# Two transformer blocks in split float32: low halves of the weight tiles written over the raw tiles, eight slots instead of four

## The chip, the cores and the metric

The kernel runs on one core of one Trainium2 chip. The metric is the device time of one execution in microseconds. Engines are named as in the profile: PE (TensorE; PEld is its weight load), DVE (VectorE), ACT (ScalarE), POOL (GpSimd), SP (SyncE, which here only issues DMAs).

## What is computed

The input x has 256 tokens of width 1024. A first block adds three attentions (differential, latent with top-k, block) and a squared-ReLU feed-forward; two further layers add a gated convolution and a retention each. Cut to what matters:

```
u = rmsnorm(x) * (1 + scale1) + shift1           # 1024 wide
p = u @ w_in                                     # 6312 columns: q, k, v, gates ...
merged = g0 * (diff_attn @ w_a) + g1 * (dsa @ w_b) + g2 * (moba @ w_c)
x = x + gate1 * (merged @ w_o)
h = square(relu(u2 @ w_ff1));  x = x + gate2 * (h @ w_ff2)      # 1024 -> 4096 -> 1024
for l in range(2):                               # two mixing layers
    p = rms_norm(x) @ w_in_2[l]                  # 1024 -> 8192: conv b, c, x, z; retention q, k, v, z
    x = x + rms_norm(concat(conv, retention) @ w_out_2[l])
```

All weights and inputs are float32.

## The kernel before

**Units.** Every weight matrix is cut into 291 units of 128 x 1024 (eight blocks of 128 x 128), in one stream in the order of use: 0 to 26 projections, 27 to 50 gates, 51 to 58 the three branch outputs, 59 to 66 w_o, 67 to 98 w_ff1, 99 to 130 w_ff2, then 80 units for each mixing layer (from 131 and from 211): 32 for the retention, 32 for the convolution (163 to 194, 243 to 274), 16 for the output. Activations lie transposed, 128 rows of 256 tokens.

**Split.** A weight tile `raw` is split into `w_hi` (ACT copies it to the matmul's rounded float32) and `w_lo = raw - w_hi`. Activations are split the same way. A unit is then eight times three matmuls, hi by hi, hi by lo, lo by hi (lines 544 to 546, and 562 to 564 in `first_units`, which runs two or three units side by side behind a norm).

**Rings.** `raw` has four slots of two tiles each (`RAW_PAIRS`), `w_hi` and `w_lo` four slots of one tile each (`SLOTS`). For unit c:

- SP loads the pair p = c // 2 (`load`, line 393). From p = 4 on it waits until the low halves of the pair four back are made.
- ACT makes the high half (`high`, line 996) when the tile has landed and unit c-4 is done. It is called at the end of ACT's work on unit c-4: `high(None, c + SLOTS)`.
- The low half (`low`) is made by POOL (line 455, four quarters of 128 x 256) and, where c % 4 == 3 and for unit 4, by DVE (line 1397, one instruction). It waits for the high half and for unit c-4.
- PE waits for both halves, and for the PSUM bank (`taken`).

```
            act.wait_ge(raw_in[(c // 2) % RAW_PAIRS], lin(g, 16, 16 * (c // 2 // RAW_PAIRS + 1)))
            if c >= SLOTS:
                act.wait_ge(S["unit_done"], lin(g, 8, c - SLOTS + 1))
```

**Order around it.** Each engine runs one program written out in order, with semaphores between them. ACT and DVE step from unit to unit: wait for `unit_done`, take the result out of PSUM, do the step's share of attention, norms, gates or activation, then `high` or `low` for a unit ahead. In the convolution stage ACT's fourth step of a group of four first waits for DVE's `zr` to take a tanh (line 1355) and then calls `high`. POOL does almost nothing but low quarters. SP does the loads in order; ten of the loads of `ada` (modulation weights) at the start and the bias table go through it as well, 14 more `ada` loads through ACT's queue.

Of the kernel before, what the change touches and what calls it, by code (L numbers as in the profile page):

```python
# [32 lines left out]
P = 128  # L33
# [33 lines left out]
SLOTS = 4  # L67
# [7 lines left out]
RAW_PAIRS = 4  # L75
# [50 lines left out]
def _build(nc, ctx, xT, weights, ada, c_row, cols, dl, relb, onehot, ident_d, flip_d, cmask_d, decay, positions, w_uv, out):  # L126
# [173 lines left out]
    names = """ident_in tab_in dl_in pos_in start_pool pool_own raw_in0 raw_in1 raw_in2 raw_in3 small_in x_in tab_out bias_in decay_in stored  # L300
# [15 lines left out]
    raw_in = [S[f"raw_in{i}"] for i in range(RAW_PAIRS)]  # L316
# [72 lines left out]
    def _(sp):  # L389
# [3 lines left out]
        def load(g, p):  # L393

            src = weights[p] if g is None else weights[bass.ds(g * 4 + p, 1)].rearrange("o p n -> p (o n)")
            if p >= RAW_PAIRS:
                n = 2 * p - 2 * RAW_PAIRS + 2
                sp.wait_ge(S["lo_pool"], lin(g, 8, n))
                if n % 4 == 0 and p > 5:
                    sp.wait_ge(S["lo_dve"], lin(g, 8, n))  # L400
                if p == 6:
                    sp.wait_ge(S["lo_first"], 1)
            both = 2 * p + 1 < UNITS
            width = (2 if both else 1) * KC * P
            sp.dma_start(raw[:, p % RAW_PAIRS, 0:width], src[:, 0:width]).then_inc(raw_in[p % RAW_PAIRS], 16)

# [5 lines left out]
        load(None, 0)  # L412
        ada_load(sp, 3)
        load(None, 1)
# [5 lines left out]
        load(None, 2)  # L420
        load(None, 3)
# [5 lines left out]
        load(None, 4)  # L427
        ada_load(sp, 8)
        ada_load(sp, 9)
        load(None, 5)  # L430
# [6 lines left out]
        for p in range(6, 8):  # L437
            load(None, p)
        n_loops = (UNITS // 2 - 8) // 4
        with sp.Fori(0, n_loops) as g:  # L440
            for i in range(4):
                load(g, 8 + i)
        for p in range(8 + 4 * n_loops, (UNITS + 1) // 2):
            load(None, p)
# [9 lines left out]
    def _(pool):  # L454
        def low(g, c):
            if g is None and c <= 4:
                if c == 4:
                    return
            elif c % 4 == 3:
                return  # L460
            pool.wait_ge(S["hi_ready"], lin(g, 8, c + 1))
            if c >= SLOTS:
                pool.wait_ge(S["unit_done"], lin(g, 8, c - SLOTS + 1))
            r = raw[:, (c // 2) % RAW_PAIRS, (c % 2) * KC * P:(c % 2 + 1) * KC * P]
            s = c % SLOTS
# [39 lines left out]
        lows(12, U_LAYER + LAYER_UNITS + SLOTS)  # L505
        x_adds(0)
        lows(U_LAYER + LAYER_UNITS + SLOTS, UNITS)
# [484 lines left out]
    def _(act):  # L992
# [206 lines left out]
        for n, (kind, q) in enumerate(BR_UNITS):  # L1199
            act.wait_ge(S["unit_done"], U_BR + n + 1)  # L1200
            high(None, U_BR + n + SLOTS)
# [27 lines left out]
        for j in range(KC):  # L1229
            o = O_WO + j  # L1230
            act.wait_ge(S["unit_done"], U_WO + j + 1)
            high(None, U_WO + j + SLOTS)
# [9 lines left out]
        def up_turn(g, base):  # L1242
            for i in range(8):
# [5 lines left out]
                high(g, c + SLOTS)  # L1249
# [14 lines left out]
        for j in range(KC):  # L1264
            for q in range(4):
                c = U_F2 + 4 * j + q
                act.wait_ge(S["unit_done"], c + 1)
                if c + 1 < U_LAYER:
                    high(None, c + SLOTS)
# [8 lines left out]
        high(None, U_LAYER + SLOTS - 1)  # L1278

        for l in range(LAYERS):  # L1280
# [4 lines left out]
            def a_turn(g, n0):  # L1285
# [34 lines left out]
                for i in range(8):  # L1320
# [10 lines left out]
                    high(g, c0 + i + SLOTS)  # L1331
# [13 lines left out]
            def b_turn(g, n0):  # L1345
                c0, o0 = uA + 32 + 8 * n0, oA + 32 + 8 * n0
                for e in range(2):
                    n = 2 * n0 + e
                    for i in range(4):
# [6 lines left out]
                        high(g, c0 + ii + SLOTS)  # L1356
# [15 lines left out]
            for j in range(KC):  # L1372
                for q in range(2):
# [8 lines left out]
                    high(None, c + SLOTS)  # L1382
# [10 lines left out]
    def _(dve):  # L1393
# [3 lines left out]
        def low(g, c):  # L1397
# [281 lines left out]
        for c in range(N_QKV + N_GATE):  # L1679
# [18 lines left out]
            if c:  # L1698
                low(None, c + SLOTS)
# [23 lines left out]
        for n, (kind, q) in enumerate(BR_UNITS):  # L1723
# [22 lines left out]
            low(None, U_BR + n + SLOTS)  # L1746
# [17 lines left out]
        for j in range(KC):  # L1764
# [4 lines left out]
            low(None, U_WO + j + SLOTS)  # L1769
# [10 lines left out]
        def up_turn(g, base):  # L1780
            for i in range(8):
# [7 lines left out]
                low(g, c + SLOTS)  # L1789
# [37 lines left out]
        for j in range(KC):  # L1827
            for q in range(4):
# [9 lines left out]
                low(None, c + SLOTS)  # L1838
# [8 lines left out]
        for l in range(LAYERS):  # L1847
# [4 lines left out]
            def a_turn(g, n0):  # L1852
# [35 lines left out]
                for i in range(8):  # L1888
# [5 lines left out]
                    if i == 3:  # L1894
                        if n0 == 0:
                            low(g, c0 + i + SLOTS)
# [3 lines left out]
                    if i != 3 or n0:  # L1900
                        low(g, c0 + i + SLOTS)
# [41 lines left out]
            def b_turn(g, n0):  # L1943
# [5 lines left out]
                for e in range(2):  # L1949
# [6 lines left out]
                    for i in range(4):  # L1956
# [29 lines left out]
                        low(g, c0 + ii + SLOTS)  # L1986
# [19 lines left out]
            for j in range(KC):  # L2006
                for q in range(2):
# [4 lines left out]
                    if j < KC - 1 or q == 0:  # L2012
                        low(None, c + SLOTS)
# [4 lines left out]
            low(None, uA + 79 + SLOTS)  # L2018
# [164 lines left out]
```

## Time and profile before

| | |
|---|---|
| time, median of 3 runs | 992.1 us (991.79, 992.1, 993.59) |
| profiled execution, its own time | 999.17 us |
| profiled execution, span | 997.3 us |
| mean granted TensorE clock | 0.987 |
| PE busy | 945.3 us (95%), 7758 matmuls |
| DVE / ACT / POOL busy | 656.8 / 493.3 / 727.8 us |
| DMA | 185.2 MB, 186 GB/s on the mean |

All times are microseconds from the start of the span. "Idle before" is the time in which an engine waited, with the line that released it; "issue" is waiting for nothing that the profile shows. Matmuls overlap, so the time from one's start to the next one's is what a matmul costs, not its own 0.28 us.

### The profile page before, as it was taken

How to read it: one execution, taken by the hardware profiler on the slowest of the kernel's cores; microseconds unless marked ns; L12 is line 12 of the kernel's file. 1: busy time of each engine (PE TensorE's matmuls, PEld its weight loads, DVE VectorE, ACT ScalarE, POOL GpSimd, SP SyncE). 2: the span in 40 equal slices, each digit the busy share in tenths (PEclk: the TensorE clock that was granted, in tenths of full speed). 3: DMA queues.
4: the chain of work that ended last, by engine and by line, in shares of the span. 5: the costliest groups of instructions: out<-in, count | busy, mean ns of one | idle time of the engine just before them, and what ended most of it. 6: DMA issues, size and time to landing. Idle time of an engine off the chain costs nothing. (4 is left out here: it accounts for less than half of the span.)

```text
span 997.3 us, 21947 instructions
## 1 busy us (share of the span) xinstructions
PE 945.3 (95%) x7758; PEld 920.4 (92%) x7758; DVE 656.8 (66%) x1097; ACT 493.3 (49%) x811; POOL 727.8 (73%) x894
## 2 busy tenths in 40 slices
PE   6999899999889999999999999999978999999996
PEld 6898789998888999999899999999978999999996
DVE  4979996756887654432566668885455666788823
ACT  3445567654446555454444454444543444644451
POOL 1585666668668888787676659999935666799993
PEclk9999999999999999999999999999988999999998
DMA  9985554646444546555344435555404444445531
GB/s 367 398 318 186 196 204 181 249 141 265 150 164 170 203 176 253 196 195 185 127 170 169 164 131 176 204 178 202 175 37 150 151 164 168 169 170 176 201 108 43
DMA packets 28222, 185.20 MB, mean 186 GB/s; under 512 B 3027, under 2 KB 5504, under 8 KB 6272
## 3 DMA queue, kind: packets, MB, share of 16 engines
q1 hardware_dynamic: 25832, 167.93, 46.4%
q10 hardware_dynamic: 2328, 16.40, 4.5%
q8 instruction: 43, 0.70, 0.3%
q14 instruction: 19, 0.16, 0.0%
HBM read 183.26 MB, written 1.07 MB: 185 GB/s over the span
## 5 line engine op out<-in xcount | busy, mean ns | idle before, releaser
L470 POOL TENSOR_TENSOR w_lo<-raw,w_hi 128x256 fp32r<-128x256 f32 x876 | 718.3, 856 | 244.0 <-ACT w_hi L1004 241.4
L544 PE MATMUL mm<-u_hi,w_hi 128*128 128x256 f32 x1600 | 460.4, 288 | 8.3 <-issue 8.1
L545 PE MATMUL mm<-u_lo,w_hi 128*128 128x256 f32 x1600 | 447.4, 280 | 0.0
L546 PE MATMUL mm<-u_hi,w_lo 128*128 128x256 f32 x1600 | 447.2, 279 | 0.0
L1004 ACT ACTIVATE w_hi<-raw 128x1024 fp32r<-128x1024 f32 x291 | 306.2, 1058 | 145.1 <-PE mm L546 140.3
L544 PEld LDWEIGHTS mm<-u_hi,w_hi 128*128 128x128 f32 x1600 | 304.3, 190 | 16.5 <-issue 15.8
L545 PEld LDWEIGHTS mm<-u_lo,w_hi 128*128 128x128 f32 x1600 | 302.4, 189 | 2.0 <-issue 1.9
L546 PEld LDWEIGHTS mm<-u_hi,w_lo 128*128 128x128 f32 x1600 | 302.8, 189 | 0.0
L1409 DVE TENSOR_TENSOR w_lo<-raw,w_hi 128x1024 fp32r<-128x1024 f32 x72 | 99.9, 1387 | 61.8 <-ACT w_hi L1004 59.2
L544 PE MATMUL mm<-mix_hi,w_hi 128*128 128x256 f32 x256 | 71.0, 277 | 1.7 <-DVE mix_lo L1979 1.7
L544 PE MATMUL mm<-h_hi,w_hi 128*128 128x256 f32 x256 | 71.9, 281 | 0.0
L545 PE MATMUL mm<-h_lo,w_hi 128*128 128x256 f32 x256 | 71.9, 281 | 0.0
L546 PE MATMUL mm<-h_hi,w_lo 128*128 128x256 f32 x256 | 71.9, 281 | 0.0
L546 PE MATMUL mm<-mix_hi,w_lo 128*128 128x256 f32 x256 | 70.7, 276 | 0.0
L545 PE MATMUL mm<-mix_lo,w_hi 128*128 128x256 f32 x256 | 70.7, 276 | 0.0
L544 PEld LDWEIGHTS mm<-mix_hi,w_hi 128*128 128x128 f32 x256 | 48.1, 188 | 2.2 <-DVE mix_lo L1979 2.1
L544 PEld LDWEIGHTS mm<-h_hi,w_hi 128*128 128x128 f32 x256 | 49.2, 192 | 0.0
L545 PEld LDWEIGHTS mm<-mix_lo,w_hi 128*128 128x128 f32 x256 | 48.1, 188 | 0.0
L546 PEld LDWEIGHTS mm<-mix_hi,w_lo 128*128 128x128 f32 x256 | 48.1, 188 | 0.0
L545 PEld LDWEIGHTS mm<-h_lo,w_hi 128*128 128x128 f32 x256 | 48.0, 188 | 0.0
L546 PEld LDWEIGHTS mm<-h_hi,w_lo 128*128 128x128 f32 x256 | 48.0, 188 | 0.0
L578 PE MATMUL mm<-ident,ones 128*128 128x128 f32 x264 | 35.1, 291 | 9.1 <-DMA ident<-ident_d 9.1
(292 smaller groups left out, 1354.0 us busy)
## 6 DMA issues: line engine op xcount, KB each, us to landing
raw<-weights SPq DMA_DIRECT2D x145, 1024.0 KB, 4.8
ada_raw<-ada ACTq DMA_DIRECT2D x14, 1024.0 KB, 5.2
ada_raw<-ada SPq DMA_DIRECT2D x6, 1024.0 KB, 12.3
ada_more<-ada SPq DMA_DIRECT2D x4, 1024.0 KB, 12.8
bias<-tab_scratch SPq DMA_DIRECT2D x1, 1536.0 KB, 9.2
dec<-decay ACTq DMA_DIRECT2D x1, 1536.0 KB, 6.9
x<-xT SPq DMA_DIRECT2D x1, 1024.0 KB, 10.8
out<-x SPq DMA_DIRECT2D x4, 256.0 KB, 2.2
```

Source lines behind the costliest of these rows:

```text
L470: ins = nc.gpsimd.tensor_tensor(w_lo[:, s, at], r[:, at], hi[:, at], ALU.subtract)
L544: nc.tensor.matmul(dst, wh, rhs_hi(k), start=a, stop=False)
L545: nc.tensor.matmul(dst, wh, rhs_lo(k), start=False, stop=False)
L546: i = nc.tensor.matmul(dst, wl, rhs_hi(k), start=False, stop=b)
L578: nc.tensor.matmul(mm[o % 4][:, 0:P], ones[:, :], ident[:, :], start=True, stop=True)
L1004: A(w_hi[:, c % SLOTS, :], r, ACT.Copy).then_inc(S["hi_ready"], 1)
L1409: ins = V.tensor_tensor(w_lo[:, s, :], r, w_hi[:, s, :].bitcast(F32), ALU.subtract)
```

## The change

`raw` and `w_lo` become one piece of memory of eight tiles: the low half is subtracted in place. `w_hi` gets eight slots too. Of a partition, the three tensors took 8 + 4 + 4 tiles of 4 KB before, and take 8 + 8 tiles now, 64 KB both times; the small fillers of 32 bytes between them move behind them. ACT makes the high half five units ahead (`HI_AHEAD`), the low halves are still called four units ahead (`LO_AHEAD`) but wait for the high half alone. Each unit's tile is loaded by a DMA of its own, 512 KB, with one semaphore per slot, as soon as the unit eight back is done. At the start, ACT makes high half 4 before the first unit is done, and the loads of units 8 and 9 stand behind two `ada` loads instead of ahead of them.

```diff
-SLOTS = 4
+SLOTS = 8
+HI_AHEAD = 5
+LO_AHEAD = 4
...
-RAW_PAIRS = 4
...
-    keep("step_raw", [P, 8])
-    raw = keep("raw", [P, RAW_PAIRS, 2 * KC * P])
-    keep("step_w", [P, 8])
+    with ExitStack() as early:
+        raw = tile_in(early, "raw", [P, SLOTS, KC * P])
+    w_lo = keep("w_lo", [P, SLOTS, KC * P], F32R)
     w_hi = keep("w_hi", [P, SLOTS, KC * P], F32R)
-    w_lo = keep("w_lo", [P, SLOTS, KC * P], F32R)
-    keep("step_vec", [P, 8])
+    keep("step_vec", [P, 24])
...
-        def load(g, p):
-
-            src = weights[p] if g is None else weights[bass.ds(g * 4 + p, 1)].rearrange("o p n -> p (o n)")
-            if p >= RAW_PAIRS:
-                n = 2 * p - 2 * RAW_PAIRS + 2
-                sp.wait_ge(S["lo_pool"], lin(g, 8, n))
-                if n % 4 == 0 and p > 5:
-                    sp.wait_ge(S["lo_dve"], lin(g, 8, n))
-                if p == 6:
-                    sp.wait_ge(S["lo_first"], 1)
-            both = 2 * p + 1 < UNITS
-            width = (2 if both else 1) * KC * P
-            sp.dma_start(raw[:, p % RAW_PAIRS, 0:width], src[:, 0:width]).then_inc(raw_in[p % RAW_PAIRS], 16)
+        def load(g, c):
+
+            if g is None:
+                src = weights[c // 2][:, c % 2 * KC * P:(c % 2 + 1) * KC * P]
+            else:
+                src = weights[bass.ds(g * 4 + c // 2, 1)].rearrange("o p n -> p (o n)")\
+                    [:, c % 2 * KC * P:(c % 2 + 1) * KC * P]
+            if c >= SLOTS:
+                sp.wait_ge(S["unit_done"], lin(g, 8, c - SLOTS + 1))
+            sp.dma_start(raw[:, c % SLOTS, :], src).then_inc(raw_in[c % SLOTS], 16)
...
-        load(None, 2)
-        load(None, 3)
+        for c in range(4, 8):
+            load(None, c)
...
-        load(None, 4)
         ada_load(sp, 8)
         ada_load(sp, 9)
-        load(None, 5)
+        for c in range(8, 11):
+            load(None, c)
         sp.wait_ge(S["tab_out"], 16)
...
             pool.wait_ge(S["hi_ready"], lin(g, 8, c + 1))
-            if c >= SLOTS:
-                pool.wait_ge(S["unit_done"], lin(g, 8, c - SLOTS + 1))
-            r = raw[:, (c // 2) % RAW_PAIRS, (c % 2) * KC * P:(c % 2 + 1) * KC * P]
-            s = c % SLOTS
-            hi = w_hi[:, s, :].bitcast(F32)
+            r = raw[:, c % SLOTS, :]
+            lo = w_lo[:, c % SLOTS, :]
+            hi = w_hi[:, c % SLOTS, :].bitcast(F32)
...
-                ins = nc.gpsimd.tensor_tensor(w_lo[:, s, at], r[:, at], hi[:, at], ALU.subtract)
+                ins = nc.gpsimd.tensor_tensor(lo[:, at], r[:, at], hi[:, at], ALU.subtract)
...
-            act.wait_ge(raw_in[(c // 2) % RAW_PAIRS], lin(g, 16, 16 * (c // 2 // RAW_PAIRS + 1)))
-            if c >= SLOTS:
-                act.wait_ge(S["unit_done"], lin(g, 8, c - SLOTS + 1))
-            r = raw[:, (c // 2) % RAW_PAIRS, (c % 2) * KC * P:(c % 2 + 1) * KC * P]
-            A(w_hi[:, c % SLOTS, :], r, ACT.Copy).then_inc(S["hi_ready"], 1)
+            act.wait_ge(raw_in[c % SLOTS], lin(g, 16, 16 * (c // SLOTS + 1)))
+            A(w_hi[:, c % SLOTS, :], raw[:, c % SLOTS, :], ACT.Copy).then_inc(S["hi_ready"], 1)
...
+        high(None, 4)
         for c in range(N_QKV + N_GATE):
             act.wait_ge(S["unit_done"], c + 1)
             (qkv_evac if c < N_QKV else act_gate)(c)
-            high(None, c + SLOTS)
+            high(None, c + HI_AHEAD)
...
             dve.wait_ge(S["hi_ready"], lin(g, 8, c + 1))
-            if c >= SLOTS:
-                dve.wait_ge(S["unit_done"], lin(g, 8, c - SLOTS + 1))
-            r = raw[:, (c // 2) % RAW_PAIRS, (c % 2) * KC * P:(c % 2 + 1) * KC * P]
             s = c % SLOTS
-            ins = V.tensor_tensor(w_lo[:, s, :], r, w_hi[:, s, :].bitcast(F32), ALU.subtract)
+            ins = V.tensor_tensor(w_lo[:, s, :], raw[:, s, :], w_hi[:, s, :].bitcast(F32), ALU.subtract)
```

Every other call of `high` with `+ SLOTS` becomes `+ HI_AHEAD` and every call of `low` becomes `+ LO_AHEAD`, at the same place of its program.

## Rows read from the trace of the kernel before

**Rows 1.** The page's costliest groups: busy us, mean ns of one, idle us before them

```profile
L470 POOL TENSOR_TENSOR w_lo<-raw,w_hi 128x256 fp32r<-128x256 f32 x876 | 718.3, 856 | 244.0 <-ACT w_hi L1004 241.4
```

**Rows 2.** Waits of the whole span, by who waited: us in total, times, longest

```profile
POOL w_lo L470 <- ACT w_hi L1004: 241.4, 105, 19.1
...
DVE w_lo L1409 <- ACT w_hi L1004: 59.2, 33, 5.3
...
PE mm L544 <- issue: 9.4, 12, 3.5
...
SPq L405 <- POOL w_lo L470: 492.6, 96, 10.1
```

**Rows 3.** Timeline of PE: start, duration, in brackets idle before

```profile
53.09 0.36 PE L544 MATMUL mm<-u_hi,w_hi 128*128 128x256 f32 x1 [0.19 <-issue]
...
277.91 0.28 PE L546 MATMUL mm<-m_hi,w_lo 128*128 128x256 f32 x1
...
279.47 0.36 PE L544 MATMUL mm<-m_hi,w_hi 128*128 128x256 f32 x1 [1.28 <-issue]
...
304.35 0.28 PE L546 MATMUL mm<-u_hi,w_lo 128*128 128x256 f32 x1
...
304.81 0.36 PE L544 MATMUL mm<-u_hi,w_hi 128*128 128x256 f32 x1 [0.18 <-issue]
...
307.50 0.28 PE L546 MATMUL mm<-u_hi,w_lo 128*128 128x256 f32 x1
...
308.32 0.36 PE L544 MATMUL mm<-u_hi,w_hi 128*128 128x256 f32 x1 [0.54 <-issue]
...
311.02 0.28 PE L546 MATMUL mm<-u_hi,w_lo 128*128 128x256 f32 x1
...
312.63 0.35 PE L544 MATMUL mm<-u_hi,w_hi 128*128 128x256 f32 x1 [1.33 <-issue]
...
936.45 0.36 PE L544 MATMUL mm<-u_hi,w_hi 128*128 128x256 f32 x1
```

**Rows 4.** Timeline of POOL up to the starts of units 66 and 74

```profile
265.32 14.05 POOL L470 TENSOR_TENSOR w_lo<-raw,w_hi 128x256 fp32r<-128x256 f32 x12 [6.51 <-ACT w_hi L1004]
301.11 11.42 POOL L470 TENSOR_TENSOR w_lo<-raw,w_hi 128x256 fp32r<-128x256 f32 x12 [11.15 <-ACT w_hi L1004]
```

**Rows 5.** Timeline of ACT, high halves of units 63, 64, 71 and 72

```profile
260.91 1.06 ACT L1004 ACTIVATE w_hi<-raw 128x1024 fp32r<-128x1024 f32 x1 [3.98 <-PE mm L546]
...
264.18 1.06 ACT L1004 ACTIVATE w_hi<-raw 128x1024 fp32r<-128x1024 f32 x1 [1.90 <-PE mm L546]
...
298.44 1.06 ACT L1004 ACTIVATE w_hi<-raw 128x1024 fp32r<-128x1024 f32 x1
...
299.96 1.06 ACT L1004 ACTIVATE w_hi<-raw 128x1024 fp32r<-128x1024 f32 x1
```

**Rows 6.** Stretches: us; busy (count) of PE, PEld, DVE, ACT, POOL; PEclk, DMA share, GB/s

```profile
250.00:262.00 12.00, 9.36 (x62) 8.62 (x61) 9.53 (x20) 4.67 (x8) 6.89 (x8) 0.86 0.28 102
312.63:473.82 161.19, 161.19 (x1368) 161.19 (x1369) 75.11 (x102) 84.90 (x132) 133.68 (x174) 1.00 0.56 200
602.66:673.82 71.16, 69.98 (x603) 69.06 (x601) 61.26 (x94) 32.18 (x43) 69.44 (x77) 1.00 0.52 185
683.34:715.98 32.64, 32.64 (x290) 32.64 (x289) 14.30 (x15) 16.63 (x24) 29.72 (x38) 1.00 0.56 198
868.03:939.27 71.24, 70.80 (x602) 70.41 (x601) 60.79 (x94) 32.16 (x43) 68.89 (x77) 1.00 0.52 185
```

**Rows 7.** Timelines of POOL and PE in the convolution stage

```profile
643.99 10.90 POOL L470 TENSOR_TENSOR w_lo<-raw,w_hi 128x256 fp32r<-128x256 f32 x12 [0.54 <-ACT w_hi L1004]
...
648.11 0.36 PE L544 MATMUL mm<-u_hi,w_hi 128*128 128x256 f32 x1 [0.28 <-issue]
```

**Rows 8.** The instructions that write x on POOL: ns min/median/max

```profile
L492 POOL TENSOR_TENSOR x<-x,o_out x8: 722/725/922, 725.5 to 993.9; 128x256 f32<-128x256 f32 x8
```

**Rows 9.** Loads of raw between 300 and 700 us, from issue to landing

```profile
DMA to landing us min/median/max: 4.6/4.8/8.9
```

More of the change, by code:

```diff
@@ L315, in _build @@
     S = {n: sem(n) for n in names}
-    raw_in = [S[f"raw_in{i}"] for i in range(RAW_PAIRS)]
+    raw_in = [S[f"raw_in{i}"] for i in range(SLOTS)]
     taken = [S[f"taken{i}"] for i in range(4)]
@@ L412, in _ @@
         load(None, 0)
+        load(None, 1)
         ada_load(sp, 3)
-        load(None, 1)
+        load(None, 2)
+        load(None, 3)
         ada_load(sp, 4)
@@ L435, in _ @@
             .then_inc(S["bias_in"], 16)
-        for p in range(6, 8):
-            load(None, p)
-        n_loops = (UNITS // 2 - 8) // 4
+        for c in range(11, 16):
+            load(None, c)
+        n_loops = (UNITS - 16) // 8
         with sp.Fori(0, n_loops) as g:
[L441 to L444, printed above, removed]
+            for i in range(8):
+                load(g, 16 + i)
+        for c in range(16 + 8 * n_loops, UNITS):
+            load(None, c)
         for q in range(4):
@@ L1200, in _ @@
             act.wait_ge(S["unit_done"], U_BR + n + 1)
-            high(None, U_BR + n + SLOTS)
+            high(None, U_BR + n + HI_AHEAD)
             if n < 2:
@@ L1231, in _ @@
             act.wait_ge(S["unit_done"], U_WO + j + 1)
-            high(None, U_WO + j + SLOTS)
+            high(None, U_WO + j + HI_AHEAD)
             if j in (2, 4):
@@ L1268, in _ @@
                 if c + 1 < U_LAYER:
-                    high(None, c + SLOTS)
+                    high(None, c + HI_AHEAD)
                 if c == U_F2 + SIN_AT:
@@ L1277, in _ @@
             square_x(2, j, x[:, j, :], scale=col("norm_final", j))
-        high(None, U_LAYER + SLOTS - 1)
+        high(None, U_LAYER + HI_AHEAD - 1)
         for l in range(LAYERS):
@@ L1330, in a_turn @@
                         vt_copy(vt_at.index(i))
-                    high(g, c0 + i + SLOTS)
+                    high(g, c0 + i + HI_AHEAD)
                     if i in (5, 7):
@@ L1381, in _ @@
                             .then_inc(taken[o % 4], 1)
-                    high(None, c + SLOTS)
+                    high(None, c + HI_AHEAD)
             root(3 + 2 * l)
@@ L1698, in _ @@
             if c:
-                low(None, c + SLOTS)
+                low(None, c + LO_AHEAD)
             lam_steps(c)
@@ L1745, in _ @@
                 o += 1
-            low(None, U_BR + n + SLOTS)
+            low(None, U_BR + n + LO_AHEAD)
             if kind == "c":
@@ L1768, in _ @@
                 .then_inc(taken[o % 4], 1)
-            low(None, U_WO + j + SLOTS)
+            low(None, U_WO + j + LO_AHEAD)
             if j:
@@ L1788, in up_turn @@
                     .then_inc(S["hl_ready"], 1)
-                low(g, c + SLOTS)
+                low(g, c + LO_AHEAD)
         up_turn(None, 0)
@@ L1837, in _ @@
                         row_lo(2, j, nf_pre[:, j:j + 1])
-                low(None, c + SLOTS)
+                low(None, c + LO_AHEAD)
                 if q == 0 and j:
@@ L1895, in a_turn @@
                         if n0 == 0:
-                            low(g, c0 + i + SLOTS)
+                            low(g, c0 + i + LO_AHEAD)
                         decayed(0)
@@ L1900, in a_turn @@
                     if i != 3 or n0:
-                        low(g, c0 + i + SLOTS)
+                        low(g, c0 + i + LO_AHEAD)
                     if i >= 6:
@@ L1985, in b_turn @@
                             dve.wait_ge(S["yc_ready"], lin(g, 2, 8 * l + n + 1))
-                        low(g, c0 + ii + SLOTS)
+                        low(g, c0 + ii + LO_AHEAD)
                         if ii == 0 and n0 == 0:
@@ L2012, in _ @@
                     if j < KC - 1 or q == 0:
-                        low(None, c + SLOTS)
+                        low(None, c + LO_AHEAD)
                 if l == 0:
@@ L2017, in _ @@
             variance(n_out)
-            low(None, uA + 79 + SLOTS)
+            low(None, uA + 79 + LO_AHEAD)
             dve.wait_ge(S["rstd_ready"], n_out + 1)
```

10 lines of the change are left out of this document (5 added, 5 removed).

## The prediction

> **What bounds the kernel now.** I read the engine table first: TensorE is busy 945.3 of 997.3 us, so only what lets PE start a unit earlier, or makes its matmuls follow each other faster, can move the time by much. A unit is one 128x1024 weight tile: 24 matmuls, preceded by one ScalarE instruction that makes its high half and by its low half, four GpSimd instructions of 856 ns mean in three units of four, one VectorE instruction in the fourth [rows 1]. Three low tiles take GpSimd 12 x 0.856 = 10.3 us of the 11 us or so that four units take PE. The reader should see there that GpSimd is the next engine behind PE, with under 10% to spare.
>
> Next the waits. PE is hardly ever held in a way that the list can name: 9.4 us in 12 waits stand as "issue", that is, nothing that the profile shows [rows 2]. GpSimd meanwhile waits 241.4 us for high halves, VectorE 59.2 us, and SyncE waits 492.6 us for low halves before it may load [rows 2]. The loads run far ahead, so their waiting costs nothing.
>
> The "issue" waits can be named by laying the PE and GpSimd timelines on each other. GpSimd's run of 12 instructions (units 64, 65, 66) ends at 265.32 + 14.05 = 279.37, and PE, which had started its last matmul of unit 65 at 277.91, starts unit 66 at 279.47 [rows 3, 4]. The run for units 72, 73, 74 ends at 301.11 + 11.42 = 312.53 and PE starts unit 74 at 312.63; the starts at 304.81 and 308.32 are of units 72 and 73 [rows 3, 4]. So each of these is a wait for the low half, and what made it late is the high half before it: GpSimd had stood idle 6.51 and 11.15 us for it, because with four slots ScalarE may not write it before the unit four back is done.
>
> Last the pace. Matmuls of a unit follow each other at one of two steps, and stay with it until something disturbs them. From 312.63 to 473.82 are 57 units, 1368 matmuls, with no stop: 161.19 / 1368 = 0.1178 us. From 683.34 to 715.98 are 12 units, 288 matmuls (the view counts two that reach over the edge): 32.64 / 288 = 0.1133 us. Both at granted clock 1.00 [rows 6]. A unit is 2.83 us at the slow step and 2.72 at the fast one.
>
> **The change part by part.**
>
> *Work.* The count of every compute instruction stays. One 1024 KB load for two units becomes two of 512 KB: 146 issues become 291, on SyncE, which mostly waits. TensorE's instructions don't change.
>
> *High halves five units ahead instead of four.* The last unit done that ScalarE waits for before it makes tile c is c-5 instead of c-4. Where PE is fed with slack this costs and brings nothing. It counts in these places:
>
> (a) Unit 66. High half 64 starts at 264.18, behind unit 60. It moves into the slot of 63, at 260.91, 3.27 us earlier [rows 5]. GpSimd's run then starts about 262.05 instead of 265.32 and ends at 276.1, before PE needs it. The wait is 279.47 - 277.91 less one step of 0.12: **1.4 us** gained.
>
> (b) Units 72 to 74. High half 72 moves from 299.96 to the slot of 71, at 298.44: 1.52 us [rows 5]. GpSimd runs without a gap behind it, so low half 74 is ready 1.52 us sooner, and unit 74 starts at 311.1 instead of 312.63. The waits are 0.34 + 0.71 + 1.49 = 2.5 us (304.81 - 304.35, 308.32 - 307.50, 312.63 - 311.02, less a step each). **1.5 us** gained; about 1.0 us of waiting at unit 74 is left.
>
> (c) The convolution stage of both layers. There ScalarE makes the high half of every fourth unit (170, 174, ...) behind a tanh that waits for VectorE, GpSimd waits 0.54 us for it, and runs 10.90 us of the next 11.45 [rows 7]; PE waits in turn (648.11) [rows 7]. The change makes that high half one unit sooner, ahead of the tanh, and puts the one behind the tanh on VectorE's tile. GpSimd then needs 10.90 us in four units of 11.31 (slow step) or 10.87 (fast step). From 602.66 to 673.82 are 25 units in 71.16 us, in the other layer 71.24 [rows 6]. At the slow step and with no wait they take 25 x 24 x 0.1178 = 70.70: 0.46 + 0.54 = **1.0 us**. It isn't the 3 us or so of waits, since a wait here often put PE on the fast step, and PE enters this stage on the slow one. At best PE takes the fast step and GpSimd bounds it: 25/4 x 10.95 = 68.4 us, 2.8 us gained in each layer. At worst nothing.
>
> (d) The start: high half 4 is made before unit 0 is evacuated, so GpSimd's first steady run begins earlier; the wait at unit 5 stands with 0.19 us at 53.09 [rows 3]. **0.2 us**, and nothing if a later wait takes it back.
>
> (e) Pace from unit 74 on. Once disturbed, which step comes next? Waits of this kind in front of a unit number 16 in the whole trace, the first at 53.09 and the last at 936.45 [rows 3]. Behind 12 of them PE took the fast step, behind 4 the slow one, and 312.63 is one of the four [rows 6]. The 57 units from 74 on have no further wait. As (b) leaves a wait at unit 74, of another length, the step is drawn again. If it is the fast one: 1368 x (0.1178 - 0.1133) = **6.2 us** gained; if the slow one, 0. I take the fast one.
>
> *In-place subtraction.* No low half is written over its own input in the trace. The nearest row is GpSimd's add of x and o_out, written over x: 722 / 725 / 922 ns for 128x256, against a mean of 856 for the low quarter, which writes elsewhere [rows 1, 8]. I take 0. An upper bound is the 922 of that row against its median, 27% more; that would fill GpSimd everywhere (below). VectorE writes in place too, in 72 units.
>
> *Low halves no longer wait for a slot, and SyncE waits for a done unit instead of a low half.* The load of tile c now starts when unit c-8 is done and is asked for when unit c-5 is done: three units, 8.2 to 8.5 us. A 1024 KB load lands in 4.6 / 4.8 / 8.9 us [rows 9], half of it should not take longer. Hidden; what comes late by under 1 us at the worst holds only ScalarE, and PE has four units behind that. In front of SyncE's wait nothing else is queued in the loop; at the start the bias table's load now stands behind three weight loads instead of two, but needs the table's store first either way. The rule that speaks against this part is from the Trainium skill, "DMA: Bandwidth & Descriptors", section "Bandwidth": it wants transfers batched to at least 1 MiB. By the fit of its section "Anatomy of one DMA", about 2.0 us plus the bytes at 436 GB/s (given for GpSimd's queue), a half load is some 3.2 us, an estimate, so it would change the sum only if loads ran one at a time; no row shows halves in a loop.
>
> *Not touched:* low halves of VectorE are still four ahead and in the same place of its program, so waits for them stay, the longest of the "issue" waits too (3.5 us [rows 2], in front of unit 215, behind the second layer's first three).
>
> Sum: 1.4 + 1.5 + 1.0 + 0.2 = 4.1 us, with the pace of (e) 10.3 us. The profiled execution took 999.2 us by its own time, 997.3 of span and 1.9 around it, and becomes 988.9. It is 7.1 us over the median of the runs shown; I take the differences to carry over: 992.1 - 10.3 = **981.8 us**.
>
> **Rivals.** What can be told from no change is about 0.2%, 2 us either way.
>
> 1. *As above, but unit 74 leaves PE on the slow step:* 992.1 - 4.1 = **988.0**. For it: the same place is slow now. Against it: the 12 to 4 above.
>
> 2. *Hidden or eaten up:* GpSimd, once earlier, meets VectorE's two-input instructions at other moments, its quarters, 0.86 us on the mean, take 10.90 / 12 = 0.91 in rows 7, and the small gains of (a) to (c) go; or a fall of the clock takes them. Around the waits of 250 to 262 the granted clock was 0.86 on the mean, that is, in part at 1.2 GHz [rows 6]: 0.14 x 12 = 1.7 us for one such fall. With (e) slow, one more fall and half of (a) to (c) lost, 988.0 + 1.7 + 2.0: **991.7**.
>
> 3. *GpSimd becomes the bound, so the kernel gets slower.* Place: the convolution stage, 64 units. Its 12 quarters take 10.90 us of 11.31, so it decides from 11.31 / 12 = 0.943 us a quarter, 4% above now. If the in-place write costs 10%, 12 x 0.908 x 1.1 = 11.99 us for four units, 0.68 more than PE needs, x 16 = 10.9 us more; (a) and (b) go with it: 992.1 + 10.9 = **1003**. Against it rows 8. The Trainium skill ("SBUF — State Buffer", section "SBUF: two separate sides") says that a GpSimd operation and a VectorE operation with two SBUF inputs lock each other out for a whole instruction; the varying quarter agrees, and the rule gives no price to writing in place.
>
> 4. *Loads arrive late, slower.* If each half took as long as the slowest whole (8.9) and ScalarE asked at 8.2, it would be held 0.7 us in each unit, which PE doesn't feel before the four units of slack are gone. It decides only if loads are served one at a time, over 2.83 us each; with the 4.6 us of rows 9 that were 291 x 4.6 = **1340 us**. Nearly excluded: transfers moved up to 200 GB/s beside each other in rows 6.
>
> 5. *The pace turns the other way.* Units 196 to 210 and 276 to 290 run at the fast step behind a wait for VectorE. If both came out slow: 30 x 0.108 = 3.2 us more, and with (e) slow and one fall of the clock more the 4.1 us are gone and over: **993 to 995**.
>
> **Numbers.** Chances: forecast 0.42 (own range 979.5 to 985), rival 1 0.26, rival 2 0.16, rival 3 0.09, rival 4 0.01, rival 5 0.06. Low end: the forecast with one layer's convolution stage at the fast step (2.3 more). High end: rivals 2 and 5 taken in, rivals 3 and 4 left out: 979.5 to 994.5. Faster by over 0.2% (under 990.1): 0.42 + 0.26 + 0.06 of rival 2 = 0.74. Within: 0.10 of rival 2 and 0.03 of rival 5 = 0.13. Slower: 0.13.
>
> **What the profile of the changed kernel would show.** (a) no gap in front of unit 66; (b) GpSimd's run for 72 begins about 1.5 us after the first three feed-forward units end instead of 2.9, and one gap of about 1 us is left at unit 74; (c) no "issue" gaps from 603 to 674 and the like 266 us later; GpSimd's low quarter at 0.86 us mean (wrong if over 0.90); VectorE's 59 us of waiting for high halves mostly gone; half loads landing under 5 us, and no ScalarE wait for them after the first 70 us. (e) shows as the length of the 57 units: 155.0 us or 161.2. The prediction is wrong if that stretch stays slow (rival 1), or if GpSimd's idle time goes and PE's gaps grow (rival 3).

## The result and the profile after

The changed kernel takes 1011.33 us (median of 4 runs, 1010.76 to 1012.97), the kernel before 992.85 beside it (4 runs, 991.79 to 996.98). The ratio is 1.0166, 95% interval 1.0130 to 1.0202: slower by 1.7%, where 1.0% faster was forecast, and outside the range. The profiled execution took 1010.92 us by its own time, 1009.1 of span, at a mean granted clock of 0.991 (before 997.3, 0.987). The profiled execution of the kernel before is 7.1 us over its median, so the two profiles lie 11.8 us apart where the medians lie 18.5 apart: stages compared below come from one profile each.

From the page of the changed kernel, the engine table, the low halves of GpSimd and the loads:

```profile
PE 966.5 (96%) x7758; PEld 943.7 (94%) x7758; DVE 663.4 (66%) x1097; ACT 492.3 (49%) x811; POOL 749.5 (74%) x894
...
L467 POOL TENSOR_TENSOR w_lo<-raw,w_hi 128x256 fp32r<-128x256 f32 x876 | 740.0, 879 | 227.8 <-ACT w_hi L998 227.5
...
raw<-weights SPq DMA_DIRECT2D x291, 512.0 KB, 3.6
```

From its waits, the rows that answer to [rows 2], and ScalarE's wait for loads:

```profile
POOL w_lo L467 <- ACT w_hi L998: 227.5, 90, 17.9
...
DVE w_lo L1401 <- PE mm L543: 27.0, 15, 4.1
...
ACT w_hi L998 <- DMA raw<-weights: 5.5, 3, 2.1
```

and from the same view, PE's own:

```profile
PE mm L541 <- issue: 5.3, 4, 3.9
```

Most of what was said of the waits came about. PE's "issue" waits fell from 12 to 4 and from 9.4 to 5.3 us, VectorE's waits for high halves are gone from the list, the loads land in 3.6 us, and the quarter subtracted in place costs 879 ns on the mean instead of 856. Two things were not said: ScalarE waited for three loads, the last and longest 2.15 us in front of 246.12 us, where none was forecast after 70 us; and a wait in front of unit 71 grew (below). The timeline of PE at the starts of units 66, 71 and 74; in front of 66 and 74, 1.28 and 1.33 us of idle time stood before [rows 3]:

```profile
278.50 0.28 PE L543 MATMUL mm<-m_hi,w_lo 128*128 128x256 f32 x1
278.62 0.28 PE L541 MATMUL mm<-m_hi,w_hi 128*128 128x256 f32 x1
...
300.74 0.28 PE L543 MATMUL mm<-u_hi,w_lo 128*128 128x256 f32 x1
301.67 0.36 PE L541 MATMUL mm<-u_hi,w_hi 128*128 128x256 f32 x1 [0.65 <-issue]
...
310.25 0.28 PE L543 MATMUL mm<-u_hi,w_lo 128*128 128x256 f32 x1
310.98 0.36 PE L541 MATMUL mm<-u_hi,w_hi 128*128 128x256 f32 x1 [0.45 <-issue]
```

Unit 66 starts without a pause, unit 74 after 0.73 - 0.12 = 0.6 us of waiting. Unit 71 waits 0.93 - 0.12 = 0.8 us; before it was 0.2. Its low half is VectorE's, and that instruction took 1.76 us in the changed kernel and 1.22 us before. VectorE's timeline, changed kernel first, then before:

```profile
299.81 1.76 DVE L1401 TENSOR_TENSOR w_lo<-raw,w_hi 128x1024 fp32r<-128x1024 f32 x1
```

```profile
300.24 1.22 DVE L1409 TENSOR_TENSOR w_lo<-raw,w_hi 128x1024 fp32r<-128x1024 f32 x1
```

GpSimd's run of quarters now starts at 298.87 us, ahead of it, and before it started at 301.11 [rows 4], behind most of it. This is the meeting of which rival 2 spoke.

Yet PE is busy 21 us longer with the same 7758 matmuls. The stretches of [rows 6] in the changed kernel, the long one moved on by one unit, to 57 units from the start of unit 75 (us; then busy time and count of PE, PEld, DVE, ACT, POOL; granted clock, DMA share, GB/s):

```profile
250.00:262.00 12.00, 8.52 (x67) 8.07 (x67) 10.80 (x26) 4.03 (x7) 8.16 (x10) 1.00 0.37 127
313.93:478.08 164.15, 164.15 (x1370) 164.15 (x1369) 82.45 (x102) 86.19 (x134) 145.97 (x177) 1.00 0.57 193
602.66:673.82 71.16, 71.16 (x596) 71.16 (x595) 60.83 (x94) 33.17 (x45) 65.07 (x73) 1.00 0.54 181
683.34:715.98 32.64, 32.64 (x275) 32.64 (x274) 12.69 (x17) 16.52 (x26) 28.35 (x37) 1.00 0.55 179
```

1368 matmuls in 164.15 us are 0.1200 us each (the count takes in two that reach over the edge). The kernel before had 0.1178 in such a stretch and 0.1133 in the other [rows 6], where 275 matmuls now stand in the place of 290. PE is never idle in the last three stretches and the granted clock is 1.00, so nothing that it waits for is late: the matmuls themselves follow each other more slowly, in every stretch looked at. For 6984 matmuls of units that is 15 us if all of them had been at 0.1178 before and 47 if all at 0.1133; the busy time says 21. PE's idle time fell from 52.0 to 42.6 us (span less busy), and 21.2 - 9.4 is the 11.8 us by which the span grew.

PE's instructions are the same. What the change does alter for a matmul is where its operands lie, and what the other engines and the loads do beside it; experiment 4 separates the two. Three fillers of 32 bytes stood between the tensors. Before, `u_hi` and `u_lo` lay 32 bytes behind a multiple of 8192 (of a partition) and both weight rings 96 behind one: 64 bytes apart. The change puts two fillers behind the rings, and the rings lie 0 bytes apart from u. Below, "placement" is this distance. It means something only up to whole multiples of 512: of a unit's eight blocks, each weight block lies 512 bytes behind the one before and each activation block 1024, so every unit runs through the distances placement, placement - 512, placement - 1024 and so on.

### The profile page after: what moved, and what is told of

The parts are those of the page before. It is cut to its first block and busy times, and to the rows that moved or that the text cites. A ratio compares the mean times of both kernels' runs of the same rounds, so it can differ in the third digit from the quotient of the medians.

```text
span 1009.1 us, 22016 instructions
## 1 busy us (share of the span) xinstructions
PE 966.5 (96%) x7758; PEld 943.7 (94%) x7758; DVE 663.4 (66%) x1097; ACT 492.3 (49%) x811; POOL 749.5 (74%) x894
## 5 line engine op out<-in xcount | busy, mean ns | idle before, releaser
L467 POOL TENSOR_TENSOR w_lo<-raw,w_hi 128x256 fp32r<-128x256 f32 x876 | 740.0, 879 | 227.8 <-ACT w_hi L998 227.5
L541 PE MATMUL mm<-u_hi,w_hi 128*128 128x256 f32 x1600 | 466.0, 291 | 5.3 <-issue 5.3
L542 PE MATMUL mm<-u_lo,w_hi 128*128 128x256 f32 x1600 | 454.1, 284 | 0.0
L543 PE MATMUL mm<-u_hi,w_lo 128*128 128x256 f32 x1600 | 454.0, 284 | 0.0
L541 PEld LDWEIGHTS mm<-u_hi,w_hi 128*128 128x128 f32 x1600 | 308.1, 193 | 11.8 <-issue 11.2
L542 PEld LDWEIGHTS mm<-u_lo,w_hi 128*128 128x128 f32 x1600 | 308.4, 193 | 2.1 <-issue 1.9
L543 PEld LDWEIGHTS mm<-u_hi,w_lo 128*128 128x128 f32 x1600 | 308.0, 192 | 0.0
L1751 DVE TENSOR_TENSOR acc<-acc,sq 128x256 f32<-128x256 f32 (+1 forms) x24 | 17.7, 738 | 42.6 <-PE mm L543 42.6
```

The source lines that it names most:

```text
L467: ins = nc.gpsimd.tensor_tensor(lo[:, at], r[:, at], hi[:, at], ALU.subtract)
L541: nc.tensor.matmul(dst, wh, rhs_hi(k), start=a, stop=False)
L542: nc.tensor.matmul(dst, wh, rhs_lo(k), start=False, stop=False)
L543: i = nc.tensor.matmul(dst, wl, rhs_hi(k), start=False, stop=b)
L1751: ins = V.tensor_tensor(acc[:, 0:w, :], acc[:, 0:w, :], sq[:, j % 2, 0:w, :], ALU.add)
```

## The experiments

**1. The fillers alone.** Into the changed kernel the distance of 64 bytes is put back; all else stays. Into the kernel before only the shift is put.

```diff
# a1_fill64, in the changed kernel
     u_lo = keep("u_lo", [P, KC, T], F32R)
+    keep("step_raw", [P, 16])
...
-    keep("step_vec", [P, 24])
+    keep("step_vec", [P, 8])
# b1_nofill, in the kernel before
-    keep("step_raw", [P, 8])
-    keep("step_w", [P, 8])
-    keep("step_vec", [P, 8])
+    keep("step_vec", [P, 24])
```

> The changed kernel with 64 bytes of filler put back ahead of raw/w_lo, taken from behind w_hi (every other tensor stays where it is). Placement theory (the step between matmuls depends on where the weight tiles lie relative to the activations: 64 bytes of shift before, 0 in the changed kernel): the steps 0.1133 and 0.1178 us come back, about 988 to 993 us, as the waits at units 66, 72, 73 stay gone. In-place, load-size or slot-count theory: the step stays at 0.1200 us and the time at 1011 us.

Measured: 991.21 us (10 runs, 989.26 to 995.12), ratio to the kernel before 0.9943 (0.9912 to 0.9973); 20 us under the change as it was made by the medians, 22 by the ratios, by 64 bytes. The ratios are the safer measure here: the kernel before, run beside each set, took between 992.9 and 997.5 us.

> The kernel before with its two fillers of 32 bytes ahead of raw and ahead of w_hi moved behind w_lo, nothing else. Placement theory: a step of 0.1200 us throughout and about 1011 to 1015 us (the step costs about 18 us and the old waits stay). Any theory that blames the rings, the loads or the in-place write: 992.9 us, no change.

Measured: 1017.04 us (4 runs, 1014.12 to 1019.83), ratio 1.023 (1.0171 to 1.0288). Equal stretches of a1_fill64, then of b1_nofill, as above:

```profile
325.00:425.00 100.00, 100.00 (x885) 100.00 (x884) 63.72 (x75) 55.26 (x89) 100.00 (x114) 1.00 0.63 210
...
600.00:650.00 50.00, 50.00 (x427) 50.00 (x426) 42.65 (x66) 23.29 (x32) 47.56 (x53) 1.00 0.56 186
683.00:708.00 25.00, 25.00 (x223) 25.00 (x222) 10.12 (x13) 12.63 (x20) 22.81 (x28) 1.00 0.56 191
```

```profile
325.00:425.00 100.00, 100.00 (x836) 100.00 (x835) 53.53 (x72) 53.74 (x90) 81.73 (x106) 1.00 0.57 203
...
600.00:650.00 50.00, 50.00 (x419) 50.00 (x418) 42.34 (x67) 26.19 (x34) 46.08 (x52) 1.00 0.49 174
683.00:708.00 25.00, 25.00 (x210) 25.00 (x210) 12.96 (x18) 11.98 (x18) 21.42 (x27) 1.00 0.57 207
```

The fast step of 0.1133 (100.00 / 883) and the slow one (50.00 / 425 = 0.1176; counts of so short a stretch leave the last digit open) are back in the one, 0.1200 (100.00 / 834) is in every stretch of the other. The shift alone makes the old kernel as slow as the change did, by the median even slower (1.0230 against 1.0166, with intervals that overlap). Without it the change is 0.6% faster than the old kernel here; a repeat in experiment 5 gives 0.3%, with an interval that reaches to 1.0004, so a small gain is likely and not more. Rings, loads and in-place subtraction are not needed for the loss.

b1_nofill also gives the price of the in-place write. Its quarters write elsewhere; those of a2_hi4 (experiment 2) write over their input, at the same step of PE and the same lead. From the pages of the two, in this order:

```profile
L468 POOL TENSOR_TENSOR w_lo<-raw,w_hi 128x256 fp32r<-128x256 f32 x876 | 711.5, 848 | 263.5 <-ACT w_hi L1002 261.3
```

```profile
L467 POOL TENSOR_TENSOR w_lo<-raw,w_hi 128x256 fp32r<-128x256 f32 x876 | 710.6, 847 | 265.7 <-ACT w_hi L998 265.0
```

848 and 847 ns: writing over the input costs GpSimd nothing that shows. The 879 ns of the changed kernel come with the fifth unit of lead.

**2. The waits alone.** The changed kernel with its high halves four units ahead again.

```diff
-HI_AHEAD = 5
+HI_AHEAD = 4
...
-        high(None, 4)
```

> The changed kernel with high halves four units ahead again. Both theories: the step stays at 0.1200 us. If the one unit more of lead was worth the 4 us that were forecast, 1014 to 1016 us, with PE's waits at units 66 and 72 to 74 back; if it was worth nothing at this step, 1011 us.

Measured: 1015.21 us (2 runs, 1015.0 to 1015.42), 3.9 us over the changed kernel; span 1013.5 against 1009.1. PE's waits in front of units 73 and 74, gone and halved in the changed kernel, stand here again, in the timeline of PE:

```profile
313.08 0.35 PE L541 MATMUL mm<-u_hi,w_hi 128*128 128x256 f32 x1 [0.41 <-issue]
...
317.38 0.36 PE L541 MATMUL mm<-u_hi,w_hi 128*128 128x256 f32 x1 [1.20 <-issue]
```

So the high half's fifth unit of lead is worth about what (a) to (d) said in sum, 4.1 us. Term by term it isn't so; see below. These are two runs against four, from two sets; by the ratios (1.0202 and 1.0166, with overlapping intervals) the difference is 3.6 us.

**3. Other placements.** In the changed kernel, as in a1_fill64 with other sizes: 32 bytes (a3_fill32), 96 (a5_fill96), 128 (a4_fill128, where the tiles behind the rings, the halves of h and of the mix, keep their distance to the weights as in the changed kernel), and 64 between `w_lo` and `w_hi`, for the high ring alone (a6_hi_only64).

> The changed kernel with 32 bytes of filler ahead of raw/w_lo instead of 0 or 64. Placement theory doesn't say which step it takes; if any shift will do, 0.1133 or 0.1178 us and 988 to 993 us; if the shift has to be a certain size, another step again, down to 0.1200 us and 1011 us. The other theories: 1011 us.

> The changed kernel with 128 bytes of filler ahead of raw/w_lo (and all that lies behind the rings moved on by 128 bytes as well). Placement theory: either more distance is at least as good (steps 0.1133 or 0.1178 us, 987 to 993 us), or what counts repeats with the address, every 64 or 128 bytes, and the step is 0.1200 us again, 1011 us.

> The changed kernel with 96 bytes of filler ahead of raw/w_lo, none behind. If what counts repeats every 64 bytes, the result of 32 bytes, about 1004 us; if it repeats every 128 bytes or more, the step may be any between 0.113 and 0.120 us, 985 to 1011 us.

> The changed kernel with 64 bytes of filler between w_lo and w_hi: only the high halves are moved against the activations. Two of three weight loads of a triple read w_hi, one reads w_lo. If each load meets only the matmul beside it, two of three steps or one of three are spared and the mean step lies between 0.1133 and 0.1200 us, 995 to 1006 us; if one bad load sets the pace of all, 0.1200 us and 1011 us.

Measured: 1003.88 us for 32 bytes (7 runs, 1002.62 to 1005.86; ratio 1.0089, 1.0059 to 1.0118), one run each for the others: 1006.68 for 96, 1007.21 for 128, 1007.53 for 64 on the high ring. All lie between the change as made and a1_fill64. a4_fill128 and a6_hi_only64 came out between the two branches of their expectations, so neither branch is borne out by the time. Of a4_fill128 one stretch of units fed from h and one fed from u tell most:

```profile
420.00:470.00 50.00, 50.00 (x419) 50.00 (x418) 20.65 (x22) 25.77 (x33) 40.03 (x51) 1.00 0.53 180
600.00:650.00 50.00, 50.00 (x424) 50.00 (x423) 42.34 (x64) 24.59 (x34) 45.11 (x52) 1.00 0.55 187
```

The stage whose distance to the weights wasn't changed stays at 50 / 417 = 0.1199, the one whose distance was goes to 50 / 422 = 0.1185: what counts is the distance of a matmul's two operands, not where the rings lie.

**4. Matmuls alone.** Is it TensorE against itself, or against what ACT, GpSimd, VectorE and the DMAs read and write meanwhile? Two small kernels leave the whole computation out and run stretches of 96 matmuls at given placements; VectorE copies one result of 0.42 us after each, and nothing else is at work.

```diff
+            for n in range(ROUNDS * len(CONFIGS)):
+                dh, dl_ = CONFIGS[n % len(CONFIGS)]
...
+                        wh = w_hi[:, k * P + dh // 4:(k + 1) * P + dh // 4]
+                        wl = w_lo[:, k * P + dl_ // 4:(k + 1) * P + dl_ // 4]
...
+                        nc.tensor.matmul(dst, wh, u_hi[:, k, :], start=a, stop=False)
+                        nc.tensor.matmul(dst, wh, u_lo[:, k, :], start=False, stop=False)
+                        i = nc.tensor.matmul(dst, wl, u_hi[:, k, :], start=False, stop=b)
```

> This kernel leaves the whole computation out. It runs only stretches of 96 matmuls of the units' form (high weight tile by high and low activation, low weight tile by high activation, 128x256) with no other engine or DMA at work, one stretch for each of fourteen placements of the weight tiles against the activations: both tiles moved by 0, 16, 32, 48, 64, 80, 96, 128, 192, 256, 320 and 512 bytes, then only the high tile by 64, then only the low one by 64; the row of fourteen is run twice. Theory one, placement alone sets the step, TensorE against itself (its weight load against the moving data): 0.120 us a matmul at 0 bytes, about 0.118 at 32, 0.113 or 0.118 at 64, as in the whole kernels, and the same in both rounds. Rival, the step comes from what the other engines and the loads write and read beside it, and the placement only decides who meets whom: the same step at all fourteen, within 0.001 us.

> As m1_pace_alone, the whole computation left out, only the stretches of matmuls; placements in bytes, in this order, run twice: 64, 320, 0, 64, 576, 320, then high tile 320 with low 64, high 64 with low 320, 832, 384, 448, 192, 320, 352, 1088, 1344, 4160, 32, 64. It asks what m1_pace_alone left open. Theory one: the step belongs to the placement alone, so each stretch at 320 takes 0.1133 us a matmul whatever ran before it, each at 64 takes 0.1178, and 832 (320 + 512) is like 320, 576 like 64. Theory two: at 64 and 320 the same two steps are open, 0.1133 and 0.1178, and which one is taken is left to how the stretch starts; then 64 shows 0.1133 in some of its stretches, or 320 shows 0.1178.

Measured, from the start of a stretch's 25th matmul to that of its last, over 71, in ns:

| placement, bytes | step | placement, bytes | step |
|---|---|---|---|
| 0, 256, 512 | 120.0 | 192, 448 | 117.8 |
| 16, 32, 48 | 118.4 | 320, 576, 832, 1088, 1344, 4160 | 113.3 |
| 64 | 113.3 or 117.8 | 352 | 117.4 |
| 80, 96, 128, 384 | 118.5 to 118.9 | high 64, low 0 / high 0, low 64 | 122.4 / 117.8 |
| | | high 320, low 64 / high 64, low 320 | 113.3 |

Up to multiples of 512, the placements 512, 576, 832, 1088, 1344 and 4160 are 0, 64, 320, 64, 320 and 64 once more. Every placement that took 113.3 leaves 64 when divided by 256, also the two with unequal tiles. Each placement came out the same in both rounds but 64. The 25th and the last matmul of three stretches of m2_pace_alone_more in PE's timeline, at 0 bytes, at 64, and at 64 again:

```profile
45.21 0.28 PE L177 MATMUL mm<-u_hi,w_hi 128*128 128x256 f32 x1
...
53.73 0.28 PE L179 MATMUL mm<-u_hi,w_lo 128*128 128x256 f32 x1
...
56.92 0.28 PE L177 MATMUL mm<-u_hi,w_hi 128*128 128x256 f32 x1
...
64.97 0.28 PE L179 MATMUL mm<-u_hi,w_lo 128*128 128x256 f32 x1
...
227.54 0.28 PE L177 MATMUL mm<-u_hi,w_hi 128*128 128x256 f32 x1
...
235.90 0.28 PE L179 MATMUL mm<-u_hi,w_lo 128*128 128x256 f32 x1
```

8.52, 8.05 and 8.36 us over 71 are 0.1200, 0.1134 and 0.1177. The rival, that the step needs the other engines, falls: with none of them at work the steps at 0 bytes (0.120), at 32 (0.118), at 128 (0.1186) and at 64 (two steps) are those of the whole kernel. At two placements they are not. At 96 bytes a5_fill96 took 0.1200 in its long stretch, the first half of which is fed from u, and 0.1185 in the convolution stage, fed from u too; with only the high ring moved by 64, a6_hi_only64 took 0.1176 in the convolution stage and 0.122 (25 / 205) only in the output units of the first layer, not in those of the second (0.1178 by the starts of units 276 and 290), where the matmuls alone took 122.4 ns in both rounds. First two stretches of a5_fill96, then two of a6_hi_only64:

```profile
325.00:425.00 100.00, 100.00 (x836) 100.00 (x835) 57.65 (x72) 52.78 (x87) 91.85 (x109) 1.00 0.58 200
600.00:650.00 50.00, 50.00 (x424) 50.00 (x423) 42.19 (x66) 24.68 (x33) 46.05 (x52) 1.00 0.54 184
```

```profile
600.00:650.00 50.00, 50.00 (x427) 50.00 (x426) 42.50 (x65) 25.04 (x34) 46.17 (x53) 1.00 0.57 189
683.00:708.00 25.00, 25.00 (x207) 25.00 (x206) 9.63 (x13) 12.49 (x19) 20.07 (x26) 1.00 0.54 177
```

So more than one step is open at other placements than 64 too, and what the other engines add at these isn't shown. Theory two of the second kernel holds at 64, where the same instructions on the same bytes take either step: three stretches of six took 0.1133, one of them behind the slow clock at the start and two behind a stretch at 0 bytes; the other three, behind stretches of 117.8 or 118.4, took 0.1178.

**5. Is another placement better than 64?** At 320 bytes all eight stretches had taken 0.1133. So:

```diff
# a9_fill320, in a1_fill64 (which runs again beside it as a10_fill64_again)
-    keep("step_raw", [P, 16])
+    keep("step_raw", [P, 80])
```

> As a1_fill64 with 320 bytes ahead of the ring in place of 64; the halves that lie behind the rings keep the place that they have in a1_fill64. In the kernels of matmuls alone all stretches at 320 bytes took 0.1133 us a matmul, whatever ran before, while 64 bytes took 0.1133 or 0.1178. Theory one, placement is all there is to it: the stages fed from u (the projections, the first feed-forward matrix, the convolution stage of both layers) go to 0.1133; the convolution stage, 64 units at 0.1178 in a1_fill64, gives back up to 64 x 24 x 0.0045 = 6.9 us, cut by GpSimd, which needs 10.9 us for every four units and PE then 10.87: 983 to 987 us. Rival, the step that a stage takes is left to how it is entered, at 320 as at 64, and the kernels of matmuls alone only happened on one side: the same as a1_fill64, 989 to 993 us, with stages at 0.1178.

> a1_fill64 once more, on the same chip as a9_fill320, so that the two can be compared: 0.994 of the kernel before, the convolution stages at 0.1178 us a matmul again.

Measured: 320 bytes 991.91 us (10 runs, 986.91 to 998.87), ratio 0.9982 (0.9945 to 1.0018); 64 bytes 991.19 (10 runs, 989.92 to 995.51), ratio 0.9973 (0.9942 to 1.0004): no difference between the two is shown. From a9_fill320, a stretch of the convolution stage of each layer:

```profile
600.00:650.00 50.00, 50.00 (x427) 50.00 (x426) 42.57 (x65) 22.79 (x30) 47.56 (x53) 1.00 0.56 185
...
875.00:925.00 50.00, 50.00 (x427) 50.00 (x426) 42.51 (x65) 21.61 (x29) 47.55 (x54) 1.00 0.57 189
```

Both are 50 / 425 = 0.1176: the slow step is there at 320 bytes too. (The output units are fed from the mix, which lies behind the rings and moved with them, so they don't test 320.) The theory that 320 is always fast is refuted. The rival is what remains, for both sizes: the step that a stage takes is left to how it is entered. What in the entry decides isn't shown.

**6. More lead still.** a1_fill64 with high halves six and low halves five units ahead, and `high(None, 5)` at the start.

> The changed kernel with the 64 bytes of filler, and high halves six, low halves five units ahead. Theory: what is left of waits for weights are VectorE's low halves 135 and 215, in front of which PE stood 1.1 and 3.8 us; they are made before the norm now, so 3 to 5 us under the run with 64 bytes of filler alone. Rival: ScalarE now asks for a tile two units after its load was issued, 5.5 us, and is held where the load takes longer (up to 6 us beside the modulation weights), and 1 us or nothing is gained.

Measured: 992.38 us (11 runs, 990.29 to 998.36), ratio 0.9948 (0.9916 to 0.9980), against 0.9943 for a1_fill64. The waits at units 71, 135 and 215 went and the time did not: in the profiled execution (span 996.6, mean granted clock 0.982 against 0.984 of a1_fill64, 992.8) units 59 to 74 took 59.6 us at a mean granted clock of 0.94, where a1_fill64 needed 55.4 at 1.00. Behind unit 211, where the wait at unit 215 went, it took 5.8 us less than a1_fill64 (table below). From single profiles it isn't shown that the lead causes the loss in front.

The starts of units in PE's timelines give the stages, in us; the last column ends with the span:

| | start of unit 75 | 75 to 131 | 131 to 211 | 211 to end |
|---|---|---|---|---|
| before | 315.5 | 158.3 | 253.2 | 270.3 |
| the change | 313.9 | 161.3 | 259.1 | 274.8 |
| b1_nofill | 319.1 | 161.3 | 260.0 | 271.8 |
| a2_hi4 | 320.3 | 161.3 | 260.4 | 271.5 |
| a1_fill64 | 314.7 | 152.3 | 252.9 | 272.9 |
| a10_fill64_again | 312.2 | 152.3 | 252.9 | 274.4 |
| a9_fill320 | 309.9 | 152.3 | 252.9 | 269.7 |
| a8_fill64_ahead6_5 | 325.0 | 152.3 | 252.1 | 267.1 |

## Why the prediction was wrong

**The step that failed** is the one under "Work": "TensorE's instructions don't change". They don't, but their operands move, and the diff said so: the fillers go behind the rings. I took this as nothing, and no rival had it. It costs (1.0166 - 0.9973) x 992 to (1.0166 - 0.9943) x 992, 19 to 22 us, twice the whole forecast gain. Two things in the trace and the kernel of before could have led there: the two steps themselves, which nothing on other engines explained, and small tensors named `step_` whose only effect is on placement. Rival 5, "the pace turns the other way", allowed a worse draw among the two known steps, 3.2 us, and not a third step of 0.1200.

**(a) to (d), the waits.** The mechanism was right, the sizes were not. (a): unit 66 starts without a gap at 0.1200, but at 64 bytes 0.67 - 0.11 = 0.6 us of waiting is left in a1_fill64, so 0.9 of the 1.4 us came. (b): at units 72 to 74 0.6 us is left where 1.0 was forecast, but unit 71 now waits 0.8 us instead of 0.2, which the forecast didn't have.

(c) brought nothing in the change as made: at 0.1200 the convolution stage takes 93.1 us for 32 units with four units of lead or five (b1_nofill and the changed kernel alike), since GpSimd has slack enough there, busy 46.08 of 50 us in b1_nofill. At 64 bytes it is 91.3 us against 91.8 and 91.9 before, 0.5 us or so in each layer: the 1.0 us of the forecast, which is for both. (d) was not tried by itself.

Together: 4.1 us forecast; 3.9 by a2_hi4 against the changed kernel (4.4 in span), and by the changed kernel against b1_nofill 3.1 in span and 5.7 between the medians. That these lie about 4.1 is in part luck. The table shows where the profiles differ: 5.2 and 6.4 us are won by unit 75, and 3.0 and 3.3 are given back behind unit 211, where the changed kernel was granted 0.93 of the clock from 720 to 790 us and the two others 0.95. Of what is won by unit 75, 2.3 us are in unit 59, the first of w_o, which takes 6.95 us in both kernels with four units of lead and 4.69 in the changed one, and which no term had; (a) gives 1.1 and 0.6 us, (b) with unit 71 about 0.8. With one profile each, these parts are less certain than their sum.

**(e), the draw of the step.** It could be seen only with the placement restored. In a1_fill64 the units from 74 on run at 0.1133, as forecast: 152.3 us from 75 to 131 against 158.3, 6.0 gained of 6.2. It came out the same way in a8_fill64_ahead6_5, a9_fill320 and a10_fill64_again. But the whole kernel won 5.7 us by the ratio of a1_fill64 and 2.7 us by that of a10_fill64_again, not 10.3. The table says where some of it went: behind unit 211 a1_fill64 takes 2.6 us more than before. From 720 to 760 us, behind the first layer's end, the kernel before and then a1_fill64 show:

```profile
720.00:760.00 40.00, 33.91 (x249) 33.09 (x249) 21.23 (x46) 16.55 (x32) 19.88 (x26) 0.87 0.21 79
```

```profile
720.00:760.00 40.00, 35.65 (x242) 34.79 (x242) 20.20 (x42) 14.22 (x28) 19.34 (x23) 0.83 0.28 93
```

The granted clock is 0.83 against 0.87 (0.84 in a10_fill64_again): 0.04 x 40 = 1.6 us of full clock lost. The same by units, from the start of unit 211 to that of unit 214, the first three units of the second layer, in the same order:

```profile
727.02:740.66 13.64, 13.64 (x105) 13.64 (x105) 5.96 (x17) 5.30 (x16) 2.74 (x3) 0.87 0.00 1
```

```profile
719.95:736.74 16.79, 16.79 (x105) 16.79 (x105) 5.96 (x18) 5.18 (x16) 2.73 (x3) 0.70 0.00 1
```

PE is busy throughout, with the same count, and takes 3.2 us longer at 0.70 of the clock; a9_fill320, granted 1.00 there, took 12.12 us. Units 12 to 26 took 64.3 us at 0.95 in a1_fill64 and 61.3 at 1.00 before, another 3.0. That is rival 2's fall of the clock, in other places than the prediction had it. Of the 10.3 us the profiles show 997.3 - 992.8 = 4.5, and these two places lost 6.2, where 5.8 are missing. But units 59 to 65 won 5.4 in the same profile, of which the forecast had 1.4, so the account doesn't close place by place. Single profiles don't show that the change causes the falls.

**In-place subtraction** at nothing: right, 847 ns in place and 848 elsewhere. The mean quarter of the changed kernel rose by 3%, far from the 10% of rival 3, and GpSimd was idle for 164.15 - 145.97 = 18 us of the long stretch. At the fast step there was no such slack: a1_fill64 shows GpSimd busy for 100.00 of the 100 us from 325 on (experiment 1), without a pause of PE. **Loads** hidden: right but for the 2.15 us at 246 us, 3.6 us to land, so rival 4 is out.

Had the fillers stayed where they were, 992.1 x 0.9943 to 992.1 x 0.9973 = 986.4 to 989.4 would have been the time: rival 1's number, 988.0, though by another sum: (e) came, and about as much went elsewhere. A hit on 988.0 would have been luck.

## What to carry to other kernels

A diff that moves, resizes or reorders tensors can change the pace of every matmul that reads them: compute each operand's byte offset before and after, and where the distance between a matmul's two operands changes, give that edit its own term. When PE is busy all the time and slower, divide a stretch without gaps by its count of matmuls before looking at any wait; then undo the layout alone, which is one line. And where two steps are seen for the same instructions, an edit that shifts a wait can draw them anew in the stage behind it.

## What the runs showed of the hardware

- The step between matmuls of 128x128 by 128x256 (float32 rounded) depends on the byte distance of weight tile and activation tile in a partition: 120.0 ns at 0, 256 and 512 bytes, 118.4 at 16 to 48, 117.8 or 113.3 at 64. No other engine is needed for it. The Trainium skill ("SBUF — State Buffer", section "SBUF: two separate sides") has it that PE never waits on anyone; no run here goes against that for other engines, but PE alone loses 6% of its step by placement (120.0 against 113.3 ns). The Trainium skill ("TensorE: Matmul & The Clock Gate", section "Step-by-step: what each phase is for") says that the weight load does not take read bandwidth from the running matmul; the table of experiment 4 goes against that, if, as the placement suggests, it is these two that meet. The meeting itself no row shows.
- At 64 bytes two steps are stable, 4% apart, for the same instructions and bytes; at 96 bytes, and with the high ring alone moved by 64, whole kernels show two as well (0.1200 and 0.1185, 0.1176 and 0.122). In the matmuls alone at 64, behind a stretch at 0 bytes the fast one came both times, behind a stretch at 32 or 48 bytes the slow one all four times; at 320 bytes the matmuls alone took the fast one eight times of eight, and the whole kernel took the slow one in its convolution stages all the same. What decides is open.
- The change of high tile and low tile by different amounts is not symmetric: 122.4 ns with only the high tile moved by 64, 117.8 with only the low one.
- Writing a 128x256 float32 subtraction over its own input cost GpSimd nothing that shows: 847 ns in place (a2_hi4), 848 elsewhere (b1_nofill), 876 instructions each.
